# Expert weights of a mixture-of-experts layer loaded in 8 KB runs: four consecutive rows a partition for gate and up, halves of rows for the down matrix

## What is computed

```python
def hierarchical_moe(h, ...):
    ...                       # top-1 of 4 groups, then top-2 of its 4 experts: combine (512, 16)
    out = jnp.zeros_like(t)
    for e in range(N_EXPERTS):                                    # 16
        hid = jax.nn.silu(t @ w_exp_gate[e]) * (t @ w_exp_up[e])   # (512, 1024) @ (1024, 512)
        out = out + combine[:, e:e + 1] * (hid @ w_exp_down[e])    # (512, 512) @ (512, 1024)
    return out.reshape(b, s, d)
```

## Time and profile before

| | |
|---|---|
| time, median of 3 runs | 1011.85 us |
| the 3 runs | 1008.75, 1016.39, 1011.85 us |
| span of the profiled execution | 1007.2 us |
| the profiled execution's own time | not given; the runs lie 1.6 to 9.2 us above its span |
| TensorE (PE) busy | 911.5 us, 90% |
| VectorE (DVE) / ScalarE (ACT) busy | 569.3 us, 57% / 494.8 us, 49% |
| expert stage, from the first row transpose on | 690.7 us to the end |
| matmul of 512 columns in this stage, start to start | 0.227 us |
| split to `whi` on ACT / to `wlo` on DVE | 1.917 us / 2.290 us each |
| mean granted TensorE clock | 0.949 |

### The profile page before, as it was taken

How to read it: one execution, slowest core, us unless ns; L and a number is a source line. 1 busy time by engine, 2 the same in 40 slices (tenths; PEclk the granted TensorE clock), 3 DMA queues, 4 the chain that set the end, 5 groups by cost and what they waited for, 6 DMA issues and landing times.

```text
span 1007.2 us, 11388 instructions
## 1 busy us (share of the span) xinstructions
PE 911.5 (90%) x4127; PEld 703.1 (70%) x4127; DVE 569.3 (57%) x669; ACT 494.8 (49%) x594; POOL 104.2 (10%) x103
## 2 busy tenths in 40 slices
PE   3999998999999999999999999815999999999993
PEld 2776665566787776778888888504888888877772
DVE  5544437733445365532424442642889989887881
ACT  5487534433524443322323231303788888876870
POOL 5000000000000000010000000032113122131010
PEclk9999999999989797799999999966999999999997
DMA  8221211211121111143223438473999999999991
GB/s 264 89 85 42 83 42 43 84 42 43 43 84 42 43 42 42 42 49 120 84 92 118 167 115 298 184 263 105 322 372 373 358 373 357 375 373 357 373 314 34
DMA packets 85562, 169.44 MB, mean 168 GB/s; under 512 B 9081, under 2 KB 10258, under 8 KB 85522
## 3 DMA queue, kind: packets, MB, share of 16 engines
q1 hardware_dynamic: 76080, 145.89, 41.1%
q0 software_dynamic: 5280, 17.88, 7.0%
q10 hardware_dynamic: 4162, 5.13, 1.5%
HBM read 155.23 MB, written 13.66 MB: 168 GB/s over the span
## 4 chain that ended last, share of the span: by engine, by line
PE 61%; DMA 17%; issue 7%; DVE 6%; ACT 6%; POOL 1%; SPq 0%; DVEq 0%; ACTq 0%; POOLq 0%
PE bank L1625 16%; PE bank L1627 16%; PE bank L1626 16%; DMA mstage<-in_w_exp_down 6%; DMA mstage<-in_w_exp_up 5%; DMA mstage<-in_w_exp_gate 4%; PE bank L1753 2%; PE bank L1731 2%; PE bank L1822 1%; PE bank L1801 1%; ACT whi L596 1%; PE bank L1740 1%; PE bank L1721 1%; PE bank L1796 1%; POOL slots L785 1%
## 5 line engine op out<-in xcount | busy, mean ns | idle before, releaser
L609 DVE TENSOR_TENSOR wlo<-mstage,whi 128x2048 fp32r<-128x2048 f32 x96 | 218.5, 2290 | 41.0 <-ACT whi L596 40.3
L596 ACT ACTIVATE whi<-mstage 128x2048 fp32r<-128x2048 f32 x96 | 183.9, 1917 | 47.8 <-PE bank L1627 32.7
L609 DVE TENSOR_TENSOR wlo<-stage,whi 128x2048 fp32r<-128x2048 f32 (+1 forms) x40 | 89.6, 2241 | 116.0 <-ACT whi L596 115.4
L1625 PE MATMUL bank<-hTh,whi 128*128 128x512 f32 x368 | 154.5, 420 | 0.0
L1627 PE MATMUL bank<-hTh,wlo 128*128 128x512 f32 x368 | 146.6, 398 | 0.0
L1626 PE MATMUL bank<-hTl,whi 128*128 128x512 f32 x368 | 146.4, 398 | 0.0
L596 ACT ACTIVATE whi<-stage 128x2048 fp32r<-128x2048 f32 (+1 forms) x40 | 74.9, 1873 | 86.6 <-PE bank L1627 80.5
L1625 PE MATMUL bank<-whi,xTh 128*128 128x512 f32 x256 | 104.2, 407 | 2.3 <-DVE xTl L1567 1.6
L1627 PE MATMUL bank<-whi,xTl 128*128 128x512 f32 x256 | 101.1, 395 | 0.0
L1626 PE MATMUL bank<-wlo,xTh 128*128 128x512 f32 x256 | 100.8, 394 | 0.0
L1625 PEld LDWEIGHTS bank<-hTh,whi 128*128 128x128 f32 x368 | 71.2, 194 | 16.9 <-issue 3.6
(11 more groups left out here) (345 smaller groups left out, 1433.7 us busy)
## 6 DMA issues: line engine op xcount, KB each, us to landing
mstage<-in_w_exp_gate SPq DMA_DIRECT2D x32, 1024.0 KB, 12.3
mstage<-in_w_exp_up SPq DMA_DIRECT2D x32, 1024.0 KB, 13.5
mstage<-in_w_exp_down SPq DMA_DIRECT2D x32, 1024.0 KB, 11.8
stage<-in_w_in SPq DMA_DIRECT2D x28, 1024.0 KB, 4.9
stage<-in_w_branch SPq DMA_DIRECT2D x6, 1024.0 KB, 4.9
stage<-in_w_out SPq DMA_DIRECT2D x4, 1024.0 KB, 5.0
xin<-in_x SPq DMA_DIRECT2D x4, 512.0 KB, 5.3
x<-in_x SPq DMA_DIRECT2D x4, 512.0 KB, 5.0
```

What stands on the lines that cost most here:

```text
L596: nc.scalar.activation(whi[:, s, :, 0:n], source_of(u)[:, :, 0:n], ACT.Copy).then_inc(hi_ready, 1)
L609: nc.vector.tensor_tensor(wlo[:, s, :, 0:n], source_of(u)[:, :, 0:n], whi[:, s, :, 0:n].bitcast(F32), ALU.subtract).then_inc(lo_ready, 1)
L1625: t.matmul(out, lhs[0], rhs[0], start=start, stop=False)
```

## The change

The data in each buffer stand differently, and what reads them follows.

- **Gate and up** (`up_src`): partition p takes the four consecutive rows 4p to 4p+3 of its half, 8 KB in one run of DRAM, in place of four rows that lie 128 rows apart. To match, `turn_rows` transposes every fourth column of `xg` (a step of 16 bytes) in place of 128 neighbours.
- **Down** (`down_src`): a unit is now 256 *rows* of the down matrix over all 1024 columns, two consecutive rows of 4 KB a partition, in place of 512 rows by 512 columns. `turn_hid` transposes every second column of `hid` (a step of 8 bytes).
- **`down_product`**: each down unit now carries six matmuls for bank 2 and six for bank 3; both banks are summed over both units. A new count `down_used` tells the splits that the first of the two units has been used; `full[2]` and `full[3]` are raised in the second.

The loads, the splits, the numbers of matmuls and transposes and the orders on ACT and DVE are as many and as before.

```diff
@@ wait_unit @@
-                which, n = ((unit_used, NB + 9 + 2 * i), (full[0], B0[0] + i + 1), (full[2], B0[2] + i),
+                which, n = ((unit_used, NB + 9 + 2 * i), (full[0], B0[0] + i + 1), (down_used, i),
                             (full[3], B0[3] + i), (unit_used, NB + 10 + 2 * i), (full[1], B0[1] + i + 1))[k]
@@ up_src, down_src @@
-                    return w[e, kh * 512:(kh + 1) * 512, :].rearrange("(j p) n -> p j n", p=P)
+                    return w[e, kh * 512:(kh + 1) * 512, :].rearrange("(p j) n -> p j n", p=P)
...
-                    return w_exp_down[e, :, nh * 512:(nh + 1) * 512].rearrange("(j p) n -> p j n", p=P)
+                    return w_exp_down[e, rows_c, :].rearrange("(p j) (a n) -> p (j a) n", p=P, n=UW)
@@ down_product @@
-                for nh in range(2):
-                    pe.wait_ge(free[2 + nh], after(m, per, B0[2 + nh] + n))
-                    ins = expert_unit(u + nh, whole(2 + nh), (hdh, hdl), True, True, m=m, per=uper)
-                    ins.then_inc(full[2 + nh], 1)
+                for kh in range(2):
+                    su = (u + kh) % RING
+                    pe.wait_ge(lo_ready, after(m, uper, u + kh + 1))
+                    for nh in range(2):
+                        if kh == 0:
+                            pe.wait_ge(free[2 + nh], after(m, per, B0[2 + nh] + n))
+                        for j in range(2):
+                            q = 2 * kh + j
+                            ins = passes(whole(2 + nh), (hdh[:, q, :], hdl[:, q, :]),
+                                         (whi[:, su, 2 * j + nh, :], wlo[:, su, 2 * j + nh, :]), q == 0, q == 3)
+                        if kh == 1:
+                            ins.then_inc(full[2 + nh], 1)
+                    if kh == 0:
+                        ins.then_inc(down_used, 1)
@@ turn_rows, turn_hid @@
-                        ins = t.transpose(bank[b][:, q * P:(q + 1) * P], xg[:, par, k * P:(k + 1) * P], ident[:, :])
+                        ins = t.transpose(bank[b][:, q * P:(q + 1) * P], xg[:, par, half * 512 + q:half * 512 + 512:4],
+                                          ident[:, :])
...
-                    ins = t.transpose(bank[6][:, j * P:(j + 1) * P], hid[:, j * P:(j + 1) * P], ident[:, :])
+                    c = 256 * (j // 2) + j % 2
+                    ins = t.transpose(bank[6][:, j * P:(j + 1) * P], hid[:, c:c + 255:2], ident[:, :])
```

More of the change, by code:

```diff
@@ L503, in build @@
         mstaged = [sem(f"mstaged{k}") for k in range(12)]
-        hi_ready, lo_ready, unit_used = sem("hi_ready"), sem("lo_ready"), sem("unit_used")
+        hi_ready, lo_ready, unit_used, down_used = sem("hi_ready"), sem("lo_ready"), sem("unit_used"), sem("down_used")
         pool_step, dve_step, act_step, idx_step = sem("pool_step"), sem("dve_step"), sem("act_step"), sem("idx_step")
@@ L570, in wait_unit @@
                 i += 1
-                which, n = ((unit_used, NB + 9 + 2 * i), (full[0], B0[0] + i + 1), (full[2], B0[2] + i),
+                which, n = ((unit_used, NB + 9 + 2 * i), (full[0], B0[0] + i + 1), (down_used, i),
                             (full[3], B0[3] + i), (unit_used, NB + 10 + 2 * i), (full[1], B0[1] + i + 1))[k]
             elif u < U_OVF:
-                b = 2 + u - (U_OVF - 2)
-                which, n = full[b], B0[b] + NEXP
+                which, n = ((down_used, NEXP), (full[3], B0[3] + NEXP))[u - (U_OVF - 2)]
             else:
@@ L579, in wait_unit @@
                 which, n = ((unit_used, NB + 9 + 2 * i), (full[0], B0[0] + i + 1), (unit_used, NB + 10 + 2 * i),
-                            (full[1], B0[1] + i + 1), (full[2], B0[2] + i + 1), (full[3], B0[3] + i + 1))[k]
+                            (full[1], B0[1] + i + 1), (down_used, i + 1), (full[3], B0[3] + i + 1))[k]
             items = 1 if ovf else 2
@@ L592, in split_hi @@
             if U_OVF <= u < U_OVF + RING:
-                act.wait_ge(full[u - U_OVF + 1], after(m, 1, B0[u - U_OVF + 1] + NEXP))
+                which, count = ((full[1], B0[1] + NEXP), (down_used, NEXP), (full[3], B0[3] + NEXP))[u - U_OVF]
+                act.wait_ge(which, after(m, 1, count))
             elif u >= RING:
@@ L659, in up_src, with down_src @@
                 if isinstance(e, int):
-                    return w[e, kh * 512:(kh + 1) * 512, :].rearrange("(j p) n -> p j n", p=P)
-                return w[bass.ds(e, 1), kh * 512:(kh + 1) * 512, :].rearrange("o (j p) n -> p (o j) n", p=P)
-            def down_src(e, nh):
+                    return w[e, kh * 512:(kh + 1) * 512, :].rearrange("(p j) n -> p j n", p=P)
+                return w[bass.ds(e, 1), kh * 512:(kh + 1) * 512, :].rearrange("o (p j) n -> p (o j) n", p=P)
+            def down_src(e, kh):
+                rows_c = slice(kh * 256, kh * 256 + 256)
                 if isinstance(e, int):
-                    return w_exp_down[e, :, nh * 512:(nh + 1) * 512].rearrange("(j p) n -> p j n", p=P)
-                return w_exp_down[bass.ds(e, 1), :, nh * 512:(nh + 1) * 512].rearrange(
-                    "o (j p) n -> p (o j) n", p=P)
+                    return w_exp_down[e, rows_c, :].rearrange("(p j) (a n) -> p (j a) n", p=P, n=UW)
+                return w_exp_down[bass.ds(e, 1), rows_c, :].rearrange("o (p j) (a n) -> p (o j a) n", p=P, n=UW)
             def item(u, e, before, m=None):
@@ L1979, in turn_rows @@
                     for q in range(4):
-                        k = 4 * half + q
-                        ins = t.transpose(bank[b][:, q * P:(q + 1) * P], xg[:, par, k * P:(k + 1) * P], ident[:, :])
+                        ins = t.transpose(bank[b][:, q * P:(q + 1) * P], xg[:, par, half * 512 + q:half * 512 + 512:4],
+                                          ident[:, :])
                     ins.then_inc(full[b], 1)
```

## The result

| | before | after |
|---|---|---|
| time, median of the runs of one comparison | 1012.5 us (4 runs) | 1023.0 us (4 runs) |
| ratio, 95% interval | | 1.0112 [1.0070, 1.0154] |
| span of the profiled execution | 1007.2 us | 1021.9 us |
| first transposes of rows at | 690.7 us | 694.7 us |
| from there to the end | 316.5 us | 327.2 us |

The changed kernel is about 1.1% slower, and the interval leaves out no change. The two spans differ by 14.7 us, but 4.0 of that lie ahead of the expert stage, in code that the change does not touch. Over all profiles of this study the stage's first transposes start between 690.7 and 696.8 us. So the stage's own length is what to compare: 10.7 us longer.

The account below looks back on a forecast made before the run. PE's own work and an equally long ring through ACT and DVE were taken to bound the turn, loads the end. Ring 19.5 - loads 8.4 = +11.1 us; 1011.85 + 11.1 - 0.5 = 1022.5 us, range 1006 to 1032.

Parts of the forecast that it names:

- The ring: Chain down product, ACT's copy and split, DVE, hid, transposes: bank 2 1.36 us later an item, 19.1 to 19.8 us in all.
- The links: Waits and work through ACT, DVE and PE in one turn: 2.99 + 0.73 + 1.94 + 7.99 + 0.90 + 3.21 = 17.76 us.
- From there DVE does not stop: 7.99: DVE from a low part at 809.15 to hid at 817.14, claimed without a gap: 7.99 us.
- The 0.90 from hid to the transposes: From hid's start on DVE at 817.14 to PE's transposes of hid at 818.04: 0.90 us.
- rival 2: PE's transposes: stepped weight loads are slow; 1028 us if hid's doubled, 1037 if the rows' took four times as long; chance 0.12.
- The loads leave the path: Expert loads: items last 19.06 us, loads 19.93, the buffers cover the rest, so 8.4 us come off.
- The bound of 8.4 us: End of the expert stage: last transposes at 984.43 in place of 976.0, all that faster loads can give back.
- The 0.5 us taken off for the spread of the runs: Run spread may partly come from the end hanging on loads, which no longer count: 0.5 us off the time.
- longer runs are worth nothing to 5%: Expert loads: 4 KB rows of x at the start against mixed 2 KB rows, 341 against 350 GB/s per DMA share.
- Rival 1: The ring does not bind: PE keeps 17.7 us a turn, faster loads return up to 8.4 us, 1003.5 us; chance 0.12.
- Rival 3: Expert loads: 8 KB runs change nothing or slow them, 1040 us at 22 us an item; chance 0.03.
- The likely case: The forecast itself, 1022.5 us, own range 1017 to 1027; chance 0.73, split 0.41 slower and 0.32 the same.

Follow-up runs that it names:

- late_word: Kernel before with only full[2] raised six matmuls later, at the 18th of the down product; 1020.5 us, ratio 1.0083 to the kernel before.
- late_word_9: Kernel before with full[2] raised nine matmuls later, at the 21st of the down product; 1030.6 us, one run.
- swap: Changed kernel with ACT's split of up 1 moved ahead of the copy of bank 2; 1007.8 us, ratio 0.9947 to the kernel before.
- loads_only: Kernel before with only the sources of the expert loads changed, so products use wrong rows; 1003.5 us, ratio 0.9896.
- flat: Changed kernel with transposes of neighbouring columns again, so products use wrong columns; 1021.5 us, ratio 1.0088 to the kernel before.
- stored_permuted: Changed kernel with the split of up 1 ahead of bank 2's copy, and hid and h stored in the new order; 1009.6 us, ratio 0.9981 to the kernel before.

## Why the prediction was right

- **The ring**. Right. Turns of 19.06 were forecast and 19.0 came; ACT's idle before pad was to be 1.7 us and was 1.75. late_word, late_word_9 and swap tie it to the one word: later by six and nine matmuls, and read later. The sum was +11.1 us; the stage grew by 10.7, or 10.4 up to the last transposes. 1022.5 was forecast and 1023.0 measured.
- **Two small errors that cancel.** The slack of the ring was taken as 0 to 0.05 us; it is 0.15 (17.55 against 17.70). The links were added up around one whole turn, and such a sum gives the turn whatever the slack is; the slack hides inside the links. "From there DVE does not stop: 7.99" held 0.13 us of it: the same stretch takes 7.86 in the changed kernel (820.57 to 828.43). The 0.90 from hid to the transposes held 0.09 (now 0.81). The step of the transposes was taken as free; it costs 0.10 us a turn, so rival 2 was there, with 1.7 us in all in place of the 5 to 15 it was given. 17.55 + 1.36 + 0.10 = 19.01. That the forecast comes within 0.5 us is luck in these sizes; the mechanism is not.
- **The loads leave the path.** Right: no wait for a load is left at the end. The bound of 8.4 us on what faster loads can give was good too: up to the last transposes, where it was worked out, loads_only gives 8.3. In its whole stage it gives 7.3. The ring's part, after against loads_only up to the same place, is then 304.1 - 285.4 = 18.7 us, where 19.1 to 19.8 was forecast. The 0.5 us taken off for the spread of the runs has no run that shows it.
- **What longer runs are worth.** Mis-sized. "By these rows longer runs are worth nothing to 5%": the rows compared a few 4 KB rows at the start with the mixed traffic of the stage, and the first are no measure of the second. Longer runs are worth 1.0 us of 19.9 an item, 5%, the very edge of what was allowed. By the Trainium skill ("DMA: Bandwidth & Descriptors", section "Why small descriptors are slow (HBM only)") the estimate was 3.4%; the direction agrees and the measured gain is larger. The error did not touch the forecast, since the late word held a turn at 19 us: late_word and flat are equal with the old loads and the new.
- **Rival 2's rule.** The Trainium skill ("Advanced Engine Details and Errata", section "SBUF Cachelines") makes hid's step of 8 bytes free and the rows' step of 16 not. The trace has 208 and 209 ns for the two, against 140 and 145 without a step: both pay, and alike, and the measurement decides. A load grows by some 65 ns, but eight transposes in a row by 0.08 us in all; why so much of it stays hidden was not tried.
- **Rival 1** falls: the ring bound, and had 0.15 us of slack. Rival 3 falls as well: no load is waited for.
- **A misread row.** The page's row of PE has twelve slices for the stage, not thirteen: the slice in which it starts, at 690.7 us, reads 5. Nothing was worked out from it.

The likely case was put at the edge of a 1% loss, and the result lies there: the interval of the ratio holds 1.01.

## What to carry to other kernels

When a product is cut another way, ask of each partial result not how long it takes but when its last piece comes, and who stands behind its reader in an in-order queue. Here a copy that nobody hurried for held up a split that everybody waited for. A new semaphore that frees a slot early is of no use to an engine that sits at an earlier wait. Nor does a sum around one turn measure a ring's slack; delaying one word by a known amount does. And take a change apart before judging it: the half that loads gate and up in long runs wins 1%, the half that cuts the down matrix anew loses about 2% (1.0112 against 0.9895).

## What the runs showed of the hardware

- Loads of 1 MB with 128 runs of 8 KB, each one packet, ran 5% faster under full load than with 512 of 2 KB (18.9 against 19.9 us an item of six loads, gathers and scatters beside them, in loads_only and before).
- A weight load of 128 fp32 columns took 140 to 145 ns from neighbours and 208 to 209 ns with a step of 8 or 16 bytes (flat and after); eight transposes in a row took 0.87 us in place of 0.79.
- A product on VectorE of 128x512 took 1.08 us in place of 0.68 with stepped operands (stored_permuted and before).
- The part ahead of the expert stage, the same code in all kernels but stored_permuted, ended between 690.7 and 696.8 us. Single spans of this kernel are no measure of half a per cent; the length of the stage and, better, of a turn are.
